# Delta inverse: the transposed block inverse is written by GpSimd and placed by transfers of ScalarE's queue, and the first turn on TensorE is left out

## What is computed

```
decay = exp(where(causal, G[..., :, None] - G[..., None, :], -inf))
tri   = where(strict, beta[..., :, None] * kk * decay, 0.0) + eye(CHUNK)
sol   = triangular_solve(tri, rhs, lower=True, unit_diagonal=True)
...
v_new = u_c - w_c @ S ;  o = qd_c @ S + qk_c @ v_new ;  S = cd_c * S + kd_c^T @ v_new
```

## Time and profile before

| | |
|---|---|
| median of 3 runs | 3077.05 us |
| the profiled execution's own time | 3075.49 us |
| its span (first to last instruction) | 3073.8 us |
| TensorE busy | 3019.0 us, 98% |
| VectorE busy | 1912.0 us, 62% |
| ScalarE busy | 1122.5 us, 37% |
| GpSimd busy | 575.0 us, 19% |
| mean granted TensorE clock | 0.995 |
| delta heads in the span | about 1725 to 2330 us |

### The profile page before, as it was taken

One profiled execution on the slowest core, in us unless ns is written; L12 is line 12 of the kernel. 1 busy time (PEld: TensorE's weight loads), 2 busy tenths in 40 slices (PEclk: granted clock), 3 DMA queues, 4 the chain that ended last, 5 costly groups with the idle time before them and its releaser, 6 DMA issues.

```text
span 3073.8 us, 41028 instructions
## 1 busy us (share of the span) xinstructions
PE 3019.0 (98%) x14498; PEld 2470.1 (80%) x14498; DVE 1912.0 (62%) x2278; ACT 1122.5 (37%) x1608; POOL 575.0 (19%) x1023
## 2 busy tenths in 40 slices
PE   8999999999999999998999999999999999999998
PEld 6888888878888888887787788888887788877886
DVE  6545454557776767677435666666655455567776
ACT  4112121245454545445224444444543111123333
POOL 1000000024443434444023222222212000000000
PEclk9999999999999999999999999999999999999999
DMA  3111111121121211112512211111121354576552
GB/s 103 49 48 48 48 48 43 46 96 42 34 55 27 55 38 44 48 34 69 185 48 49 93 38 38 38 38 38 38 79 55 118 184 143 184 260 219 192 191 83
DMA packets 326887, 252.50 MB, mean 82 GB/s; under 512 B 79496, under 2 KB 282248, under 8 KB 326544
## 3 DMA queue, kind: packets, MB, share of 16 engines
q1 hardware_dynamic: 325648, 251.28, 26.5%
q10 hardware_dynamic: 1152, 0.07, 0.0%
HBM read 187.31 MB, written 64.00 MB: 82 GB/s over the span
## 4 chain that ended last, share of the span: by engine, by line
PE 92%; DVE 3%; issue 1%; POOL 1%; ACT 1%; DMA 1%; SPq 0%; DVEq 0%; POOLq 0%; ACTq 0%
PE banks L887 12%; PE banks L889 12%; PE banks L888 12%; PE banks L990 9%; PE banks L992 9%; PE banks L991 9%; PE banks L1432 3%; PE banks L1433 3%; PE banks L1434 3%; PE banks L1020 2%; PE banks L1266 1%; PE banks L1033 1%; PE banks L1035 1%; PE banks L1034 1%; PE banks L1012 1%
## 5 line engine op out<-in xcount | busy, mean ns | idle before, releaser
L990 PE MATMUL banks<-state_a_hi,weights_hi 128*128 128x512 f32 x1296 | 549.0, 424 | 1.3 <-DVE projection_staged L2050 1.1
L991 PE MATMUL banks<-state_a_lo,weights_hi 128*128 128x512 f32 x1296 | 511.8, 395 | 0.0
L992 PE MATMUL banks<-state_a_hi,weights_lo 128*128 128x512 f32 x1296 | 511.6, 395 | 0.0
L1463 ACT ACTIVATE weights_hi<-weights_raw 128x1024 fp32r<-128x1024 f32 x194 | 204.6, 1054 | 590.2 <-PE banks L889 519.5
L1907 DVE TENSOR_TENSOR weights_lo<-weights_raw,weights_hi 128x1024 fp32r<-128x1024 f32 x194 | 262.1, 1351 | 120.5 <-ACT weights_hi L1463 117.9
L992 PEld LDWEIGHTS banks<-state_a_hi,weights_lo 128*128 128x128 f32 x1296 | 243.5, 188 | 58.7
L990 PEld LDWEIGHTS banks<-state_a_hi,weights_hi 128*128 128x128 f32 x1296 | 244.4, 189 | 43.0 <-issue 2.0
L991 PEld LDWEIGHTS banks<-state_a_lo,weights_hi 128*128 128x128 f32 x1296 | 245.1, 189 | 36.7 <-issue 0.5
L2034 DVE TENSOR_TENSOR_SCAN stick_left<-stick_left,eps_column 128x128 f32<-128x128 f32 (+1 forms) x192 | 243.5, 1268 | 39.4 <-POOL beta L737 33.6
L887 PE MATMUL banks<-state_a_hi,weights_hi 128*128 128x512 f32 x648 | 256.4, 396 | 2.3 <-DVE stream_again L2290 1.5
L889 PE MATMUL banks<-state_a_hi,weights_lo 128*128 128x512 f32 x648 | 256.1, 395 | 0.0
(11 more groups left out here) (412 smaller groups left out, 6062.1 us busy)
## 6 DMA issues: line engine op xcount, KB each, us to landing
weights_raw<-in_mlp_w_dram SPq DMA_DIRECT2D x48, 512.0 KB, 4.1
relu_blocks_dram<-relu_blocks_staged SPq DMA_DIRECT2D x16, 1536.0 KB, 6.2
weights_raw<-in_gdn_w_in_dram SPq DMA_DIRECT2D x33, 512.0 KB, 4.0
weights_raw<-in_pool_w_in_dram SPq DMA_DIRECT2D x32, 512.0 KB, 3.8
weights_raw<-in_sb_w_in_dram SPq DMA_DIRECT2D x32, 512.0 KB, 4.0
relu_blocks_dram<-relu_sums_staged SPq DMA_DIRECT2D x16, 1024.0 KB, 8.9
relu_b<-relu_blocks_dram SPq DMA_DIRECT2D x16, 1024.0 KB, 9.5
state_b_lo<-relu_blocks_dram SPq DMA_DIRECT2D x16, 1024.0 KB, 13.2
```

What stands on the lines that cost most here:

```text
L990: pe.matmul(psum[:, bank, :], whi, hi, start=(k == 0), stop=False)
L991: pe.matmul(psum[:, bank, :], whi, lo, start=False, stop=False)
L992: last = pe.matmul(psum[:, bank, :], wlo, hi, start=False, stop=(k == end - 1))
L1463: act.activation(w_hi[slot][:, :], raw[slot][:, :], ACT.Copy).then_inc(weights_hi, 1)
```

## The change

`invert_blocks` gets one more GpSimd instruction: a copy of `Xb` with its two block axes exchanged into `Nb` (event `xbT`). SyncE stores it to a second DRAM buffer. GpSimd clears `inverse_T` (event `xT0`) after the copy of `k` and after `U7`. The turned blocks are placed on the diagonal of `inverse_T` by 8 transfers which ScalarE's queue issues between `ohi` and `oln` of the head before (in the first head, 4 by SyncE and 4 by ScalarE). `T3` on TensorE and `XT3` on ScalarE go; before `Q4` TensorE waits for the transfers. As `inverse_T` is now cleared early, `squares_hi_o` moves to the memory of `q_decayed`, so VectorE's `q_decayed` waits for `osums`.

```
-        square_hi = {... (("k", oT), ("o", XT))}
+        square_hi = {... (("k", oT), ("o", qd))}
...
-        POOL_PREP = ["dsub", "maskD", "Db", "x0", "xb", "knc"]
-        PE_MAIN = (["P4", "T3", "Q4", "turn_v", ...
+        POOL_PREP = ["dsub", "maskD", "Db", "x0", "xb", "xbT", "knc", "xT0"]
+        PE_MAIN = (["P4", "Q4", "turn_v", ...
-        ACT_MAIN = ["XT3", "vn", "XT4", "XT5", "osq", "ohi", "oln", "ors"]
+        ACT_MAIN = ["vn", "XT4", "XT5", "osq", "ohi", "oln", "ors"]
...  SyncE, place_blocks
                 sp.dma_start(xb_dram.rearrange("b c r n -> (b c) r n"), Xb[:, :, :]).then_inc(inverse_saved, 16)
+                ev.wait("pool", "xbT")
+                sp.dma_start(xbT_dram.rearrange("b c r n -> (b c) r n"), Nb[:, :, :]).then_inc(inverse_T_saved, 16)
                 sp.wait_ge(inverse_saved, xbs.add(16))
...  SyncE, first head only
+            def place_turned(mine):
+                ev.wait("pool", "xT0")
+                sp.wait_ge(inverse_T_saved, 16)
+                for b in mine:
+                    r = slice(b * BLK, b * BLK + BLK)
+                    sp.dma_start(XT[r, :, r], xbT_dram[b].rearrange("c r n -> r c n"), allow_slow_non_contiguous=True).then_inc(xT_blocks, 16)
             place_blocks(range(0, NB, 2))
+            place_turned(range(0, NB, 2))
...  GpSimd, end of invert_blocks
+                ev.wait("pool", "xb")
+                pool.sem_inc(mask_begun, 1)
+                ev.did("xbT", pool.tensor_copy(Nb[:, :, :], Xb[:, :, :].rearrange("p i m -> p m i")))
+            def clear_turned():
+                pool.sem_inc(mask_begun, 1)
+                ev.did("xT0", pool.memset(XT[:, :, :], 0.0))
...  GpSimd, head
                 ev.wait("dve", f"R{TT - 1}")
                 keep_k()
+                ev.now("pe", f"U{TT - 1}")
+                clear_turned()
...  TensorE, level loop
-                    ev.did(f"T{l - 1}", turn_all(lambda c: X[:, c, :], 6))
+                    if l > LEVEL0:
+                        ev.did(f"T{l - 1}", turn_all(lambda c: X[:, c, :], 6))
                     fill()
                     ev.wait("dve", f"P1_{l}")
-                    ev.wait("act", f"XT{l - 1}")
+                    if l > LEVEL0:
+                        ev.wait("act", f"XT{l - 1}")
+                    else:
+                        pe.wait_ge(xT_blocks, turned_blk.add(16 * P // BLK))
...  ScalarE
+            def place_turned(mine):
+                act.wait_ge(inverse_T_saved, xts.add(16))
+                act.sem_inc(turned_asked, 1)
+                for b in mine:
+                    r = slice(b * BLK, b * BLK + BLK)
+                    act.dma_start(XT[r, :, r], xbT_dram[b].rearrange("c r n -> r c n"), allow_slow_non_contiguous=True).then_inc(xT_blocks, 16)
...
                 ev.did("ohi", act.activation(square_hi["o"][:, :], flat(oT), ACT.Square))
+                if kind != "last":
+                    ev.wait("pool", "xT0")
+                    place_turned(range(P // BLK))
                 ev.wait("pe", "osums")
                 ev.did("oln", ...
...  VectorE
-            def q_decayed():
+            def q_decayed(summed=True):
+                if summed:
+                    ev.wait("pe", "osums")
                 ev.wait("act", "expG")
```

More of the change, by code:

```diff
@@ L209, in build @@
         last_row = place("last_row_ones", [P, P])
-        square_hi = {n: nc.alloc_sbuf_tensor_at(f"squares_hi_{n}", [P, S], F32R, offset=x.manual_sbuf_range[0]) for n, x in (("k", oT), ("o", XT))}
+        square_hi = {n: nc.alloc_sbuf_tensor_at(f"squares_hi_{n}", [P, S], F32R, offset=x.manual_sbuf_range[0]) for n, x in (("k", oT), ("o", qd))}
         square_hi["q"] = square_hi["k"]
@@ L215, in build @@
         nb_dram = nc.dram_tensor("system_blocks_dram", (P // BLK, TT, BLK, BLK), F32).ap()
+        xbT_dram = nc.dram_tensor("inverse_blocks_T_dram", (P // BLK, TT, BLK, BLK), F32).ap()
         xb_dram = nc.dram_tensor("inverse_blocks_dram", (P // BLK, TT, BLK, BLK), F32).ap()
@@ L259, in build @@
         out_by_dve, out_by_act = sem("out_scaled_by_vector"), sem("out_scaled_by_scalar")
+        inverse_T_saved, xT_blocks, turned_asked = sem("inverse_T_saved"), sem("inverse_T_blocks"), sem("turned_blocks_asked")
         blocks_saved, blocks_back, inverse_saved, x_blocks = sem("blocks_saved"), sem("blocks_back"), sem("inverse_saved"), sem("x_blocks")
@@ L276, in build @@
         ACT_PREP = ["sqk", "khi", "expD", "k_ln0", "k_ln1", "k_root", "expG", "sqq", "qhi", "q_ln0", "q_ln1", "q_root"]
-        POOL_PREP = ["dsub", "maskD", "Db", "x0", "xb", "knc"]
-        PE_MAIN = (["P4", "T3", "Q4", "turn_v", "P5", "T4", "Q5", "P6", "T5", "Q6"]
+        POOL_PREP = ["dsub", "maskD", "Db", "x0", "xb", "xbT", "knc", "xT0"]
+        PE_MAIN = (["P4", "Q4", "turn_v", "P5", "T4", "Q5", "P6", "T5", "Q6"]
                    + [f"{x}{c}" for c in range(TT) for x in "KUS" if c or x != "K"] + ["osums"])
@@ L1212, in scores @@
                 ev.did("scores", last)
-            blk = Tally()
+            blk, turned_blk = Tally(), Tally()
             def out2_tile(between):
@@ L1278, in head @@
                     if l == LEVEL0:
-                        pe.wait_ge(silu_done, v_silu[0])
+                        pe.wait_ge(silu_done, ev.head * 4 + 3)
                         ev.now("dve", "kdec")
@@ L1325, in head @@
                     assert at_hop[0] == HOPS
-            v_silu = [0]
             pe.wait_ge(mean_rounded, 1)
@@ L1344, in _ @@
             head("first")
-            with turns(pe, HEADS - 2, [(tile, 4), (half, 8), (blk, 16 * P // BLK)]) as e:
+            with turns(pe, HEADS - 2, [(tile, 4), (half, 8), (blk, 16 * P // BLK), (turned_blk, 16 * P // BLK)]) as e:
                 ev.head = e + 1
-                v_silu[0] = 4 * e + 3
                 head("full")
             ev.head = HEADS - 1
-            v_silu[0] = 4 * HEADS - 1
             assert half.fixed % 4 == 2
@@ L1673, in norm_roots @@
                 ev.did(f"{which}_root", act.activation(flat(squares), flat(squares), ACT.Exp, scale=-0.5))
+            xts = Tally()
+            def place_turned(mine):
[4 more added lines that the diff above has]
+                    act.dma_start(XT[r, :, r], xbT_dram[b].rearrange("c r n -> r c n"), allow_slow_non_contiguous=True).then_inc(xT_blocks, 16)
             def round_mixed(k):
@@ L1719, in head @@
                 for l in range(LEVEL0, LEVELS):
-                    ev.wait("pe", f"T{l - 1}")
-                    ev.did(f"XT{l - 1}", copy3(flat(XT), bl(6)))
-                    if l == LEVEL0:
+                    if l > LEVEL0:
+                        ev.wait("pe", f"T{l - 1}")
+                        ev.did(f"XT{l - 1}", copy3(flat(XT), bl(6)))
+                    else:
                         ev.wait("pe", "turn_v")
@@ L1772, in _ @@
                 act.dma_start(X[r, :, r], xb_dram[b].rearrange("c r n -> r c n"), allow_slow_non_contiguous=True).then_inc(x_blocks, 16)
-            with turns(act, HEADS - 1, [(tile, 4), (landed[0], 32), (landed[1], 32), (halves, 8), (sl_in, 1), (cd_in, 3), (sdn, 4)]) as e:
+            ev.wait("pool", "xT0")
+            place_turned(range(1, P // BLK, 2))
+            ev.prep = 1
+            with turns(act, HEADS - 1, [(tile, 4), (landed[0], 32), (landed[1], 32), (halves, 8), (sl_in, 1), (cd_in, 3), (sdn, 4), (xts, 16)]) as e:
                 ev.head = e
@@ L2418, in _ @@
             scores_decayed()
-            q_decayed()
+            q_decayed(False)
             evac(0)
```

## The result

The changed kernel took 3082.07 us, the median of 20 runs (3079.03 to 3084.77). The kernel before took 3075.61 on the same chip, the median of 20 runs (3074.07 to 3079.55). The ratio of the runs taken in pairs is 1.0016, with a 95% interval of 1.0011 to 1.0022. That is about 4.9 us more: the interval leaves out 1, but the loss is small, and the two medians by themselves differ by 6.5. The profiled execution took 3079.11 us (span 3077.4), 3.6 more than the profiled execution before.

The account below looks back on a forecast made before the run. TensorE was taken as the bound almost everywhere, except before `Q4`, where it waits for `P1_4`. Terms of 1.8, 1.0, 0.3 and -0.8 gave +2.3 us on the 3077.05 median: 3079.4 us, own range 3077 to 3083, 8-in-10 range 3074.5 to 3087.5.

Parts of the forecast that it names:

- The place of the turn: Before `Q4`, which waits for `P1_4`: removing `T3`'s 0.88 us was taken as 0 in passages 0, 2, 3, 4 and 5.
- ScalarE's issues hold `oln`: Eight issues, 3.64 us, ahead of `oln`: ScalarE free 6.4 us after the end of `xb`, `oln` late by 0.04 to 1.74.
- The rival in which the issues hold nothing: Ahead of `oln`: the issues do not delay it, only gains of 1.7 us remain, giving 3075.4 us; chance 0.14.
- the 0.78 us: Between the end of `oln` and `P4`: 0.78 us of cover, so TensorE itself loses nothing earlier.
- The sum at `Q4`: Seven passages: 1.8 us for passages 0, 2, 3, 4, 5, 1.0 for passage 1, 0.3 for passage 6.
- its late reload: Passage 1: a late reload made `xb` 1.3 us later; without it 0.45 - 0.70 instead of +1.0, total +1.0.
- `q_decayed`'s wait: On VectorE, `q_decayed` waits for `osums` and moves by 0.3 us, over before `y1` can start; taken at nothing.
- SyncE's placing: On SyncE's queue behind the new store: 0.7 us of cover, so the eight placings of `inverse` do not move.
- The late second store: Rival: the turned blocks' store is seen late, moving `oln` in seven passages; 1.2 us more gives 3087.8; chance 0.18.
- The clock: Rival: TensorE's longer wait before `Q4` drops its clock, costing 3 us per passage, 21 in seven, giving 3100; chance 0.04.
- The wait: TensorE before `Q4`: waits 0.12 + 0.88 + 0.2 to 0.45 us more, given as 1.5 to 2 us in all.
- The first head: First head, TensorE at half clock: the removed turn is worth 0 to 1.76 us, taken as 0.8 us gained.

Follow-up runs that it names:

- e2_by_sync: The changed kernel with all eight transfers of the turned blocks issued by SyncE behind those of `inverse`, none by ScalarE outside the first head: 3077.75 us, ratio 1.0003.
- e3_half: The changed kernel with four of the turned blocks' transfers issued by SyncE and four by ScalarE in every head: 3077.45 us, ratio 1.0000.
- e1_turn_kept: The changed kernel with the turn `T3` back on TensorE, its result unused: 3085.86 us, ratio to before 1.0030.
- e11_four_more: The changed kernel with four more unused 8 KB DRAM-to-DRAM transfers on ScalarE's queue behind the eight in seven passages: 3115.84 us, ratio to before 1.0127.
- e4_wait_alone: The kernel before with only `squares_hi_o` moved to the memory of `q_decayed`, which then waits for `osums`: 3076.79 us, ratio 0.9997.
- e7_after_again: The changed kernel timed once more, with no further edit: 3083.80 us, ratio to before 1.0021.
- e6: The kernel before, turn kept, with only `P1_4` of the next head moved between `y1` and `y2`: 3074.75 us, ratio 0.9995.
- e8: Repeat of e1_turn_kept, the changed kernel with `T3` back on TensorE and its result unused: 3085.35 us, ratio to before 1.0026.
- e5: e3_half with VectorE's `P1_4` of the next head moved ahead, between `y1` and `y2`: 3072.11 us, ratio to before 0.9983.
- e9: The changed kernel with 16 unused transposes between `P4` and `Q4` of the last head alone: 3081.54 us, ratio to before 1.0014.
- e10: e5 with eight unused transposes more in the last head: 3069.55 us, ratio to before 0.9975.

## Why the prediction was right, and where its sizes were off

The forecast was 3079.4 us by the median, 2.3 over before, in a range of 3077 to 3083. Measured were 3082.07 and, by the ratio, 4.9 over before. The mechanism up to `Q4` was right; the term that was mis-sized is the clock behind it.

*The place of the turn.* `T3` was priced at nothing in front of a wait for `P1_4`. That is shown: `e2_by_sync` and `e3_half` have the removal without the late `oln` and gain 0.1 us per head; `e1_turn_kept` has `Q4` of passage 0 at the same distance with the turn as without it. What 0.88 us of TensorE's work became is in the bracket before `Q4`: 0.19 us of idle time before, 1.19 after.

*ScalarE's issues hold `oln`.* Predicted 6.4 us after the end of `xb`, measured 6.68 in all seven passages. The parts: transfers begin after 2.86 (predicted 2.7, the turned copy took 0.62 for my 0.45), they last 3.71 (3.64), and the hand-over is 0.11 (0.05). The Trainium skill (DMA: Bandwidth & Descriptors, "Issuing engines are not separate DMA queues") calls the sequencer's time to initiate a transfer usually small relative to the transfer itself. One issue here is: 0.46 us against 1.8 from issue to landing, the median of the 60 transfers of L1703. What did not hold is what the prediction drew from it, a cost not worth counting: eight issues stand one behind another, 3.71 us, on an engine of the chain. Undoing only the choice of queue (`e2_by_sync`) brought `oln` back to 7.94 and took back the loss as far as the intervals tell, and four more issues (`e11_four_more`) moved `oln` by another 2.5 us. The rival in which the issues hold nothing fell with it. One reading was wrong without harm: TensorE did lose time earlier. `P4` waits for `oln` and began 0.3 to 0.7 us later after `oT` (10.24 instead of 9.84 in passage 0; passage 1 aside), as little of the 0.78 us was cover: `P4` begins 0.4 to 0.8 us after the end of `oln` even when it waits for it. At `Q4` nothing of it is seen, since `P1_4` comes later still.

*The sum at `Q4`.* Predicted 1.8 + 1.0 + 0.3 = 3.1 us over the seven passages, measured 2.89. So close a sum is luck, as two errors cancel. Six passages cost 0.26 to 0.82 us where I had 0.04 to 0.45. Passage 1 cost -0.03 where I had +1.04, because its late reload did not come again; that case was named, at 0.45 - 0.70. `q_decayed`'s wait is nothing (`e4_wait_alone`), although one reason given was wrong: GpSimd's user of the decay row does not come later than the row but waits for it (in the kernel before `decay_matrix` begins at 1804.37, after 10.57 us of idle time that the row's landing ended). And SyncE's placing was not moved by the second store. The late second store did not happen: the clearing of `inverse_T`, not the store, set the start of the issues. It ended at 1794.69 in passage 0, with the first issue at 1794.88.

*The clock.* This is the step that failed, in its size and its form. I gave the fall 0.04, as something that comes in all seven passages or none, and argued from 1.75 us of idle time ahead of the first head that kept the full clock. In the profile of after, the wait at that very place (1.93 us, L1219 above) lost it: one wait that kept the clock was no evidence. It fell in two passages of after, behind waits of 1.19 and 2.16 us, and made 2.9 of the 5.6 us by which the heads grew. In `e7_after_again`, whose execution took 3083.80 us and so lies nearer to the medians, it fell in one passage; the heads were 8.2 us longer than before, 3.6 up to `Q4` and 4.7 behind it. The prediction's 3 us per fall was near the middle (1.3 to 4.7) by chance, as its 6 us at half clock were 3.4 in one profile and 13.7 in the other; the count was wrong.

The wait was mis-sized too. The terms given, 0.12 + 0.88 + 0.2 to 0.45, add up to 1.2 to 1.45 us and not to 1.5 to 2, and all passages were taken as alike. Measured were 0.55 to 1.19 us in passages 0 to 5, less than forecast because `P4` is late as well, and 2.16 in passage 6. The last head has less work to fill with and waited 1.21 us already before, and that is where the clock fell in both profiles of after. The profiles of all kernels, by the wait before `Q4`, show how far the wait decides:

| place | wait, us | profiles or waits | clock fell | low for, us |
|---|---|---|---|---|
| last head | 1.83 to 2.16 | after, `e2`, `e3`, `e7` | 4 of 4 | 3.4, 10.2, 6.8, 13.7 |
| last head | 1.21 to 1.28 | before, `e1`, `e4`, `e6`, `e8` | 2 of 5 (`e4`, `e8`) | 3.4, 6.8 |
| last head | 0.15 to 0.78 | `e5`, `e9`, `e10` | 1 of 3 (`e5`, after 0.78) | 3.4 |
| passage 0 | 1.17 to 1.19 | after, `e7`, `e9` | 2 of 3 | 3.4, 3.4 |
| passages 0 to 5 | 0.55 to 0.96 | 27 waits of after, `e2`, `e3`, `e7`, `e9` | none | |

So the longer waits go with more falls in the last head, 4 of 4 against 2 of 5 in few profiles, but they are not the only cause: `e4` and `e8` have the turn and lost the clock there too. With the 2.9 us of its profile put in, the forecast would have been 3.1 + 2.9 - 0.8, 5 us over before. That the timed ratio gives 4.9 proves nothing by itself, since the two profiled executions differ by 3.6 and the medians by 6.5.

*The first head.* Predicted -0.8, measured -1.43. But it lasted between 69.6 and 73.6 us over the kernels, with and without the turn (71.3 in `e1_turn_kept`, 73.6 in `e5_half_early`). The clock at its start was low for 6.8 us before and in `e1_turn_kept`, 3.4 in after and 13.7 in `e5_half_early`, enough to account for the difference. What the turn is worth there stays open.

*Also open.* What decides in which passage and execution the clock falls, and for how long: in passage 0, 1.18 us of idle time lost it, 1.17 did not. And why the late reload in passage 1 came, more or less late, only in the kernels with `T3` on TensorE (before, `e1`, `e4`, `e6` and `e8`) and in none of the others: with one profile of each it may be chance.

## What to carry to other kernels

When an engine stands in the chain that ends last, a transfer that it only issues costs its full issue time, here 0.46 us, although the profile counts it as idle. The idle time in front of a waiting instruction is room for issues only from the moment their data is ready. Before removing work from the busiest engine, look whether the next thing it does is a wait: there the work is worth nothing until the wait moves. And the lengthened wait may cost clock behind it: look first for the place where the engine already waits longest, here the last head. Remove the wait first, here by putting `P1_4` ahead of `y2`, and the removed work begins to pay.

## What the runs showed of the hardware beyond that

- A transfer of 8 KB from DRAM to DRAM held ScalarE for 0.65 us at its issue, one from DRAM to SBUF for 0.46.
- In `e3_half`, eight issues of SyncE took 3.62 us beside four of ScalarE (1.78), as long as alone: the two do not hold each other up.
- TensorE's clock fell after waits of 0.78, 1.18 and 1.21 us in some executions and kept its full rate after 1.17 and 1.21 in others. In `e2_by_sync`, 1.83 us of idle time in the last passage brought a stretch of 10 us at clock 0.55, where the kernel before had 1.00 after 1.21:

```profile
2262.00:2272.00 10.00, 9.43 (x47) 9.43 (x48) 4.12 (x6) 2.91 (x3) 0.00 (x0) 0.55 0.22 58
```

- GpSimd's turned copy took 0.61 to 0.64 us in the passages and 1.62 to 1.63 in the first head, in all ten profiles that have it. In the first head VectorE begins a run of six operations with three operands beside it; that the one stretches the other was not tested. In after:

```profile
1720.61 8.62 DVE L2238 SCALAR_TENSOR_TENSOR stream_again<-stream_again,norm_gains,v_by_token 128x1024 f32<-128x1024 f32 x6 [3.17 <-POOL inverse_blocks L848]
1720.74 1.63 POOL L851 COPY system_blocks_T<-inverse_blocks 64x256 f32<-64x256 f32 x1 [0.17 <-POOL inverse_blocks L848]
```
